# Hybrid decoder trunk: the selection mask moves from TensorE to VectorE's bias, with splits and a spread in another order

## The reference, cut to what matters

```
for l in range(2):                                          # x: 256 tokens x 1024, float32
    h = h + 0.5 * swiglu(rms_norm(h), gate, up, down)       # d_ff 2816 (22 tiles of 128)
    h = h + token_mixing(rms_norm(h), w_in, ...)
    h = h + 0.5 * swiglu(rms_norm(h), gate, up, down)
out = rms_norm(h)

# token_mixing: 8 sparse heads and 8 forgetting heads, 64 wide
score  = sum over 8 index heads of w_i * relu(q_i @ k_i)    # causal, else NEG = -1e30
idx    = top 64 of score per query
logits = q_lat @ c_kv[idx] / 8 + rel_bias[bucket(t - idx)]  # sparse heads, softmax over idx
logits = q @ k / 8 + cum[t] - cum[s]                        # forgetting heads, causal softmax
out    = concat(heads) @ w_out
```

## Time and profile before

| | |
|---|---|
| median of 3 runs | 1002.12 us (1002.12 to 1002.3) |
| the profiled execution | 1002.46 us, of which 1000.5 from the first to the last instruction |
| granted clock of TensorE, mean | 0.998 |
| busy: TensorE, VectorE, ScalarE, GpSimd | 989.8, 759.5, 538.6, 139.6 us |
| start of the first pair of heads, layer 0 and layer 1 | 247.10 and 739.33 us |

### The profile page before, as it was taken

One profiled execution on the slowest core, in us unless ns is written; L12 is line 12 of the kernel. 1 busy time (PEld: TensorE's weight loads), 2 busy tenths in 40 slices (PEclk: granted clock), 3 DMA queues, 4 the chain that ended last, 5 costly groups with the idle time before them and its releaser, 6 DMA issues.

```text
span 1000.5 us, 16509 instructions
## 1 busy us (share of the span) xinstructions
PE 989.8 (99%) x5631; PEld 842.5 (84%) x5631; DVE 759.5 (76%) x1523; ACT 538.6 (54%) x977; POOL 139.6 (14%) x155
## 2 busy tenths in 40 slices
PE   9999999999999999999999999999999999999997
PEld 8888888888878888888888888889887788888885
DVE  6887777688667887777788777777886688777775
ACT  5555555565565555555555555555755555555553
POOL 3000000018761000000000000000287500000001
PEclk9999999999999999999999999999999999999999
DMA  8665556775534655555536555554563546555541
GB/s 303 209 207 188 187 183 190 248 240 177 190 110 148 227 189 189 189 189 189 189 128 213 196 186 187 189 185 137 198 213 130 172 147 224 190 189 189 189 147 42
DMA packets 38164, 184.75 MB, mean 185 GB/s; under 512 B 3904, under 2 KB 8176, under 8 KB 23920
## 3 DMA queue, kind: packets, MB, share of 16 engines
q1 hardware_dynamic: 33408, 178.60, 54.0%
q10 hardware_dynamic: 4720, 5.67, 1.8%
HBM read 183.18 MB, written 2.64 MB: 186 GB/s over the span
## 4 chain that ended last, share of the span: by engine, by line
PE 94%; DVE 3%; POOL 1%; ACT 1%; DMA 0%; issue 0%; DVEq 0%
PE ps L645 33%; PE ps L646 17%; PE ps L639 12%; PE ps L641 12%; PE ps L640 12%; PE ps L897 1%; DVE xboth L1162 1%; PE ps L909 1%; PE ps L731 1%; POOL rstd L295 1%; PE ps L888 1%; PE ps L884 1%; DMA cst<-consts 0%; PE ps L655 0%; PE ps L659 0%
## 5 line engine op out<-in xcount | busy, mean ns | idle before, releaser
L645 PE MATMUL ps<-xboth,whi 128*128 128x512 f32 x1440 | 508.5, 395 | 0.0
L646 PE MATMUL ps<-xboth,wlo 128*128 128x256 f32 x1440 | 403.7, 280 | 0.0
L645 PEld LDWEIGHTS ps<-xboth,whi 128*128 128x128 f32 x1440 | 270.0, 188 | 64.7 <-issue 1.0
L646 PEld LDWEIGHTS ps<-xboth,wlo 128*128 128x128 f32 x1440 | 272.0, 189 | 3.5
L1120 DVE TENSOR_TENSOR wlo<-raw,whi 128x1024 fp32r<-128x1024 f32 (+1 forms) x214 | 250.6, 1206 | 5.7 <-ACT whi L386 5.7
L386 ACT CAST whi<-raw 128x1024 fp32r<-128x1024 f32 (+1 forms) x222 | 217.6, 1030 | 7.4 <-PE ps L641 7.4
L1126 DVE TENSOR_TENSOR wlo<-raw,whi 128x1024 fp32r<-128x1024 f32 (+1 forms) x110 | 132.2, 1202 | 98.8 <-ACT whi L390 98.8
L426 ACT ACTIVATE sig<-hg 128x256 f32<-128x256 f32 x88 | 36.9, 419 | 198.8 <-DVE hg L1207 182.2
L390 ACT CAST whi<-raw 128x1024 fp32r<-128x1024 f32 (+1 forms) x112 | 112.8, 1007 | 52.2 <-PE ps L641 52.0
L639 PE MATMUL ps<-whi,hhi 128*128 128x512 f32 x352 | 138.7, 394 | 0.4 <-DVE hlo L1226 0.4
L641 PE MATMUL ps<-whi,hlo 128*128 128x512 f32 x352 | 138.9, 395 | 0.0
(11 more groups left out here) (184 smaller groups left out, 1194.2 us busy)
## 6 DMA issues: line engine op xcount, KB each, us to landing
raw<-stream SPq DMA_DIRECT2D x111, 1024.0 KB, 5.1
raw<-stream SPq DMA_DIRECT2D x113, 512.0 KB, 3.6
decay<-table ACTq DMA_DIRECT2D x2, 1024.0 KB, 8.2
table<-table ACTq DMA_DIRECT2D x1, 1524.0 KB
X<-x SPq DMA_DIRECT2D x2, 512.0 KB, 5.3
bias<-table ACTq DMA_DIRECT2D x1, 1024.0 KB, 5.9
raw<-stream SPq DMA_DIRECT2D x2, 256.0 KB, 6.2
fgain<-final_gain ACTq DMA_DIRECT2D x1, 512.0 KB, 6.7
```

Of the source, the lines that this page charges most:

```text
L645: nc.tensor.matmul(ps[:, bank, :], a[0], xboth[:, k, :], start=k == 0, stop=False)
L646: return nc.tensor.matmul(ps[:, bank, 0:S], a[1], xhi[:, k, :], start=False, stop=k == KT - 1)
```

## The change

VectorE adds the mask. For each sparse head `masked(h)` writes drop times -1e30 plus bias into `lg`, in two instructions (128 and 256 columns), and `maxima` adds that instead of the bias, in place. The mask matmuls go, and with them `nident` and TensorE's wait for `drop`. Heads 0 and 1 are masked ahead of `tile_sum(7)`, 2 and 3 among the splits behind the first maxima, 4 and 5 behind `turned(1)`, 6 and 7 behind `back(8)`. The split of chunk 6 moves behind the first pair's maxima.

Besides: the latent's spread stands behind tile QI + 2 and VectorE's `back(2)` ahead of `cn`; the back part of the chunk 0 of a layer is split by GpSimd, behind the norm's `power`, and no longer by VectorE; and the eight warm-up matmuls between the transposes go. Left out below are the declarations of `nident`, `nident_set` (gone) and the semaphore `masked_out` (new).

```diff
@@ -304,11 +303,11 @@
                 nc.gpsimd.tensor_tensor(wlo[:, s, at], raw[:, s, at], whi[:, s, at].bitcast(F32),
                                         ALU.subtract).then_inc(w_front, 1)
 
-            def split_back(l, m):
-
-                k = NF + m
+            def split_back(l, k):
+
                 s, at = k % 2, slice(FRONT, CHUNK)
-                pool.wait_ge(w_back, chunk(l, k))
+                if chunk(l, k):
+                    pool.wait_ge(w_back, chunk(l, k))
                 pool.wait_ge(hi_back, chunk(l, k) + 1)
                 nc.gpsimd.tensor_tensor(wlo[:, s, at], raw[:, s, at], whi[:, s, at].bitcast(F32),
                                         ALU.subtract).then_inc(w_back, 1)
@@ -345,6 +344,7 @@
             LAST = DEPTH * 3
             for l in range(DEPTH):
                 power(l * 3)
+                split_back(l, 0)
                 if l == 0:
                     pool.wait_ge(tri_in, 16)
                     nc.gpsimd.tensor_copy(tri[:, :, :].rearrange("p b t -> p (b t)"), tri_raw).then_inc(tri_set, 1)
@@ -355,7 +355,7 @@
                 scale(l, 0, 1)
                 split_front(l, 4, 1)
                 scale(l, 1, 2)
-                split_back(l, 4)
+                split_back(l, NF + 4)
                 scale(l, 2, 3)
                 split_front(l, 5, 0)
                 scale(l, 3, 4)
@@ -732,8 +732,8 @@
                                                 X[:, b, k * P:(k + 1) * P], ident)
                         if b == NB - 1 and k % 2 == 1:
                             t.then_inc(xt_mm, 1)
-                    if n == 0:
-                        idle((8, 2)[b])
+                    if n == 0 and b == NB - 1:
+                        idle(2)
 
             def spread(bank):
 
@@ -876,17 +876,13 @@
                     elif g:
                         pe.wait_ge(feat_out, l * NTILE + (2 * h2 - 1))
                     for i in range(2):
-                        if g == 0:
-
-                            nc.tensor.matmul(ps[:, LOGB + i, 0:S3], nident[:], drop[:], start=True, stop=True)
-                    for i in range(2):
                         rows = slice(HD * i, HD * i + HD)
                         nc.tensor.matmul(ps[:, LOGB + i, 0:P], feat[rows, q, 0:P], feat[rows, key, 0:P],
-                                         start=g == 1, stop=True, skip_group_check=True)
+                                         start=True, stop=True)
                     for i in range(2):
                         rows = slice(HD * i, HD * i + HD)
                         nc.tensor.matmul(ps[:, LOGB + i, P:S3], feat[rows, q, P:S], feat[rows, key, :],
-                                         start=g == 1, stop=True, skip_group_check=True).then_inc(qk_mm, 1)
+                                         start=True, stop=True).then_inc(qk_mm, 1)
 
                 def turn(hh):
 
@@ -939,7 +935,8 @@
                 u.then_inc(feat_mm, 1)
                 tile(QI, front(1, 0), 0, lambda: spread_rows(l * 3 + 1, ROWS_MIX))
                 tile(QI + 1, front(1), UNIT, token_major)
-                tile(QI + 2, back(1), FRONT, latent_rows)
+                tile(QI + 2, back(1), FRONT)
+                latent_rows()
 
                 pe.wait_ge(tri_set, 1)
                 pe.wait_ge(logf_lo_out, l + 1)
@@ -1003,7 +1000,6 @@
                 wide_tile(6, s, FRONT)
                 wide_tile(7, front(5, 0), 0)
 
-                pe.wait_ge(drop_out, l + 1)
                 pe.wait_ge(relu_out, l * NH + NH)
                 pe.wait_ge(va_out, l * NB + NB)
                 pe.wait_ge(ka_out, (l + 1) * (QA - KA))
@@ -1177,8 +1173,6 @@
                 dve.wait_ge(diag_hi_out, n + 1)
                 diagonal_low(rstd).then_inc(diag_out, 1)
                 split_front(l, k, halves=(1,))
-                if g == G_FFN1:
-                    split_back(l, 0)
                 dve.wait_ge(rows_mm, n + 1)
                 nc.vector.tensor_copy(rows[:, :], ps[:, bank, 0:S]).then_inc(rows_out, 1)
                 dve.wait_ge(rows_out, n + 1)
@@ -1225,6 +1219,8 @@
                     dve.wait_ge(hhi_out, n + 1)
                     nc.vector.tensor_tensor(hlo[:, s, :], hf[:, s, :], hhi[:, s, :].bitcast(F32), ALU.subtract
                                             ).then_inc(hlo_out, 1)
+                    if (f, phase) == (0, 0):
+                        dve.wait_ge(w_back, chunk(l, 0) + 1)
                     if back:
                         split_back(l, k0 + f + 1, i, back)
                     if front:
@@ -1267,15 +1263,26 @@
                             nc.vector.match_replace(score[:, ats[b]], top8[:, b, :], score[:, ats[b]], TAKEN
                                                     ).then_inc(top_step, 1)
 
+                def masked(h):
+
+                    if h >= 4:
+                        dve.wait_ge(pr_out, l * 2 * NH + (h - 3))
+                    for at, n in ((slice(0, P), P), (slice(P, S3), S)):
+                        t = nc.vector.scalar_tensor_tensor(out=lg[:, h % 4, at], in0=drop[:, at], scalar=NEG,
+                                                           in1=bias[:, h, S - n:S], op0=ALU.mult, op1=ALU.add)
+                    t.then_inc(masked_out, 1)
+
                 def maxima(hh):
 
                     g, h = divmod(hh, NH)
                     s, bank = hh % 4, LOGB + hh % 2
+                    if hh < NH:
+                        dve.wait_ge(masked_out, l * NH + (hh + 1))
                     if hh == NH:
                         dve.wait_ge(decay_set, 2 * l + 2)
                     wait_apart(qk_mm, l * 2 * NH + (hh + 1), hh % 4)
                     for b, at, n in ((0, slice(0, P), P), (1, slice(P, S3), S)):
-                        add = bias[:, h, S - n:S] if g == 0 else decay[:, h, at]
+                        add = lg[:, s, at] if g == 0 else decay[:, h, at]
                         t = nc.vector.tensor_tensor_reduce(lg[:, s, at], ps[:, bank, at], add, -SCALE, -LOWEST,
                                                            ALU.add, ALU.min, nm[:, s, b:b + 1])
                     t.then_inc(lg_out, 1)
@@ -1342,9 +1349,9 @@
                 nc.vector.tensor_tensor(logf_lo[:], logf[:], logf_hi[:].bitcast(F32), ALU.subtract
                                         ).then_inc(logf_lo_out, 1)
                 front(2, (1,))
+                back(2)
                 dve.wait_ge(crows_mm, l + 1)
                 nc.vector.tensor_tensor(cn, ct, ps[:, CB, 0:S], ALU.mult).then_inc(cn_out, 1)
-                back(2)
                 dve.wait_ge(chi_out, l + 1)
                 nc.vector.scalar_tensor_tensor(out=clo[:], in0=cn, scalar=gains_all[:, l, G_CKV:G_CKV + 1],
                                                in1=chi[:].bitcast(F32), op0=ALU.mult, op1=ALU.subtract
@@ -1380,12 +1387,11 @@
                 dve.wait_ge(w_back, chunk(l, NF + 5))
                 back(5)
                 tile_sum(6)
-                dve.wait_ge(w_front, chunk(l, NF + 6) * 2)
-                front(6, (0,))
+                dve.wait_ge(bias_in, 16)
+                dve.wait_ge(drop_out, l + 1)
+                masked(0)
+                masked(1)
                 tile_sum(7)
-                front(6, (1,))
-                back(6)
-                dve.wait_ge(bias_in, 16)
                 for p in range(NPAIR + 2):
                     if p < NPAIR:
                         maxima(2 * p)
@@ -1393,18 +1399,28 @@
                     if p >= 2:
                         out_low(p - 2)
                     if p == 0:
+                        dve.wait_ge(w_front, chunk(l, NF + 6) * 2)
+                        front(6, (0,))
                         tile_out(FX + 4, FILLB)
+                        masked(2)
+                        front(6, (1,))
+                        back(6)
+                        masked(3)
+                        tile_out(FX + 5, FILLB)
                         front(7)
-                        tile_out(FX + 5, FILLB)
                     if p == 1:
                         back(7)
                         tile_out(FX + 6, FILLB)
                         turned(0)
                         tile_out(FX + 7, FILLB)
                         turned(1)
+                        masked(4)
+                        masked(5)
                     if p == 2:
                         front(8)
                         back(8)
+                        masked(6)
+                        masked(7)
                     if p == 4:
                         front(9, (0,))
                     if p == 6:
@@ -1438,7 +1454,6 @@
             nc.vector.memset(ones[:].bitcast(F32), 1.0).then_inc(ones_set, 1)
             nc.vector.memset(chi[:].bitcast(F32), 0.0).then_inc(zero_set, 1)
             dve.wait_ge(id_in, 16)
-            nc.vector.tensor_scalar(nident[:], ident, NEG, None, ALU.mult).then_inc(nident_set, 1)
             for b in range(NB):
                 dve.wait_ge(x_in[b], 16)
                 nc.vector.memset(spare[:, b:b + 1], 0.0).then_inc(x_ready, 2)
```

(5 more changed lines are left out.)

## The result

The change made the kernel slower, by less than forecast: 1004.87 us (10 runs, 1004.58 to 1005.65) against 1002.17 beside it (10 runs, 1002.07 to 1003.06), a ratio of 1.0024 (95% interval [1.0015, 1.0032]). The profiled execution took 1004.93 us with a span of 1003.1, so the span grew by 2.6, at the same granted clock of 0.998.

What follows compares the result with a forecast made beforehand. TensorE, busy 99% of the span, bounds the kernel. Terms +0.5 + 0.9 - 0.8 - 2.65 + (1.4 + 2.5) + (1.9 + 2.5) = +6.25 on 1002.12 give 1008.4 us; 8-in-10 range 998.5 to 1011.

Steps and rivals of the forecast that it cites:

- Part 1: At the start: without warm-up matmuls, but GpSimd's back split holds up diag_lo and TensorE waits for it: +0.5 us.
- Part 2: The same split in layer 1: diag_lo ends later and down(0) starts at 515.7 instead of 514.76: +0.9 us.
- Part 3: Latent spread behind the tile: the wait for diag_lo goes, chunk 2 then limits: -0.4 us per layer, -0.8 in all.
- Part 4: Mask matmuls gone from TensorE's chain, four pairs per layer at 0.33 us: -2.65 us.
- Part 5: Masks on VectorE make TensorE wait at turn(1) and turn(3): 1.4 + 2.5 us in layer 0, 1.9 + 2.5 in layer 1.
- the second deadline: turn(3) needs turned(2), with masks 4 to 7 in between: TensorE waits 2.5 us per layer.
- (a): Rival: masks dodge GpSimd, only stalls of 0.2 + 0.4 per layer stay, diag_lo still held up: 1001.3 us, chance 0.2.
- (b): Rival: GpSimd doesn't hold up operations with a scalar factor (diag_lo, masks): 998.4 us, chance 0.18.
- (c): Rival: a mask loses to several GpSimd instructions in a row, 1.4 us more once or twice per layer: 1011 to 1014, chance 0.12.

Runs made afterwards that it cites:

- the last two experiments: Changed kernel with table behind head 5, masks 6 and 7 behind turned(3), back split on VectorE, tri copy later: 1000.56 us; same with the table waiting for masks: 997.55 us.

## Why the prediction was right in its direction and wrong in its size

**Part 1** held: diag_lo ended at 18.64 (18.7 forecast) and TensorE's spread came at 18.70. The lag was 0.46 there and 0.56 one matmul later, since the second followed the first after 0.22 instead of 0.12. It was still 0.56 at `down(0)` and 0.7 to 0.8 from the next tile on; that last step has no wait beside it in the trace and stays open.

**Part 2** had the right mechanism; 1.33 was measured at `down(0)` instead of 0.94. VectorE is 2.12 late at diag_lo, as forecast (2.07); its own split of 1.13 saved leaves 0.99, and hf starts 0.89 behind ht instead of 0.53. That pause ahead of hf has no counterpart in the trace before. It stands in layer 1 of all five traces in which GpSimd splits the back part of chunk 0 (0.46 each time, also with the split behind diag_lo), and in none of the eight in which VectorE does. What it waits for isn't clear from the trace, and it was not tried.

**Part 3** held: -0.42 and -0.43, with the new wait for chunk 2. **Part 4** held: eight pairs at 0.33. The sixth split cost nothing to be seen.

**Part 5** is the step of the prediction that failed, in size and not in kind: the waits stand at the second and fourth `turn` of each layer, as forecast, but they are worth 1.97 and 1.96 instead of 3.9 and 4.4. That is 4.4 of the excess, against 0.8 that parts 1 and 2 were short. Four things made it up:

- The price of a pair, 0.67, was taken from the score sums, which have a factor per partition; it is 0.54. With four pairs ahead of each deadline that is 0.5 each time, 2.1 us over the four.
- The collisions were fewer than I counted instruction by instruction. `turned(0)` ended at 261.50; less the 0.32 by which all was late, that is 261.18, where I had 262.4. At 0.54 a pair the end without collisions would be 261.2 - 0.5 = 260.7, so the collisions cost 0.5 more than in the kernel before, not 1.2. The masks lost about what I had for them (1.83 + 0.74 + 0.53 from start to next start, less 4 x 0.54, is 0.9). What I had too small is what the splits had already lost in the kernel before. I set 0.9 against the new collisions, the back split at 257.51; but the three splits of chunk 6, ahead of the first maxima, had lost 0.2, 0.2 and 0.5 there, and the pair at 253.56 0.2. That is 2.0 in all, and 1.5 after the change. With the masks' 0.9 it makes 2.4 against 2.0. The splits of chunk 6 in the kernel before (one of 1,024 columns takes 1.22 alone, one of 8 takes 0.15):

```profile
246.41 1.43 DVE L1120 TENSOR_TENSOR wlo<-raw,whi 128x1024 fp32r<-128x1024 f32 x1
...
248.09 1.41 DVE L1120 TENSOR_TENSOR wlo<-raw,whi 128x1024 fp32r<-128x1024 f32 x1
249.42 0.69 DVE L1126 TENSOR_TENSOR wlo<-raw,whi 128x8 fp32r<-128x8 f32 x1
```

- Ahead of the second deadline front(8) lost 0.3 to the table addition instead of 1.0: it takes 1.62 there, and 1.28 in the last two experiments, where the addition is elsewhere. The addition ended at 266.31, 0.47 after front(8) was issued.
- In layer 1 I had added 0.5 for drop's late end. The waits of layer 1 are those of layer 0: after the change drop takes 0.77 there, as in layer 0. Its meeting with GpSimd is the same as before, with the first product issued 0.31 behind it, and the outcome is another. The changed kernel, then the latent spread alone on the kernel before, which has the order of the earlier trace rows:

```profile
737.91 0.77 DVE L1385 SCALAR_TENSOR_TENSOR drop<-score,cst 128x384 bf16<-128x384 f32 x1
...
738.23 3.48 POOL L318 TENSOR_TENSOR feat<-val,rows 128x256 f32<-128x256 f32 x3
...
735.28 0.82 DVE L1379 SCALAR_TENSOR_TENSOR drop<-score,cst 128x384 bf16<-128x384 f32 x1
...
735.59 6.13 POOL L319 TENSOR_TENSOR feat<-val,rows 128x256 f32<-128x256 f32 x4
```

Each of the thirteen traces has two drops, and in all 26 the product is issued 0.28 to 0.33 behind. 25 of them take 0.74 to 0.82, and only that of the earlier trace rows takes 2.20. What decides it the traces don't show; the term rested on an outcome that didn't come again.

The four come to 5.4 over both layers (2.1 + 2 x 0.7 + 2 x 0.7 + 0.5). The 0.15 that each of the four waits costs beyond its length, which I had left out, takes 0.6 back, and 0.4 stays unexplained. None of the four was tried by itself.

**The rivals.** (a), masks without collisions, gave the waits 1.2 in all, and 3.9 were measured. The two experiments on the table and on the masks' place show collisions and load both at work: the table's place alone is worth 1.55, the masks' place alone 3.0. (b), operations with a scalar factor that GpSimd doesn't hold up, is refuted by diag_hi (2.50 and 2.40 instead of 0.29) and by the masks (2.22 instead of 0.41 beside an addition). (c), a mask that loses to several GpSimd instructions in a row, didn't happen either: the longest single mask, even beside two additions back to back, took 2.22. Drop's 2.20 stays the one case seen in which an instruction of VectorE stood through more than one, once in 26 drops.

The Trainium skill ("SBUF — State Buffer", section "Who interferes with whom") has the later of the two instructions wait until the other has ended. The masks and the additions follow it, one wait for each instruction, and so do the split and `ur` above, of which each was once the later. Drop's row doesn't.

The forecast's own bound for no measurable effect was 2 us; the change cost 2.7.

## What to carry to other kernels

Work moved from the engine that bounds to one with idle time is paid at deadlines, not by its sum: here 32 mask instructions of 484 ns on the mean, 15.5 us, cost 3.9, and 3.0 of that came back when the masks of two heads per layer were put elsewhere. Look at what each deadline has ahead of it and put the new work right behind one. When two engines hold each other up, moving either one's work moves the collision; order the two with a wait where they would meet, for a wait of 1.1 us on the idle engine took away 1.33 on the one that bounds, in each layer. And take the price of an operation from a row of the same form, the kind of its factor included (0.35 with a factor per partition, 0.28 with a constant, for 128 columns), and the outcome of a meeting from more than one trace.

## What the runs showed of the hardware that was not expected

- A TensorScalar of 128x128 with one tile in SBUF and a factor per partition is held up by GpSimd's split as well: 2.50 and 2.40 instead of 0.29. I had expected this of diag_lo, with two tiles. The Trainium skill ("SBUF — State Buffer", section "Who interferes with whom") counts `tensor_scalar` among the operations that can take the shared ports, and this trace agrees.
- The pair of masks takes 0.61 with `drop` in bf16 and 0.61 in float32.
- GpSimd pays too: its table addition of 2.00 took 2.98 where it was issued at 256.65, during a split of VectorE, and its split of 2.4 took 3.33 in the run with the later split.
- The same meeting of two instructions, issued at the same distance to 0.01 us, can end either way: drop took 2.20 in the kernel before and 0.82 in the run with the latent spread alone, and 0.74 to 0.82 in the 24 other cases.
